# HGRN decay levels in a decoder step: from full 128x128 score blocks to the blocks that each mask keeps

## The reference, cut to what matters

```
def step(s, blk):
    qc, kc, vc, gc = blk
    b = jnp.cumsum(gc, axis=1)
    dec = jnp.exp(jnp.where(causal, b[:, :, None] - b[:, None, :], -jnp.inf))
    att = jnp.einsum('bthk,bshk,btshk->bhts', qc, kc, dec)
    o = jnp.einsum('bhts,bshv->bthv', att, vc) + jnp.einsum('bthk,bhkv->bthv', qc * jnp.exp(b), s)
    ...
```

## Time and profile before

| what | value |
|---|---|
| median of three runs | 3149.97 us (3140.21 to 3153.35) |
| the profiled execution | 3146.2 us |
| its span | 3144.4 us |
| mean granted TensorE clock | 0.949 |
| TensorE matmul busy | 2903.4 us (92%) |
| VectorE busy | 1385.3 us (44%) |
| ScalarE busy | 1325.0 us (42%) |
| all HGRN heads | from about 490 to 862 us of the span |

### The profile page before, as it was taken

One profiled execution on the slowest core, in us unless ns is written; L12 is line 12 of the kernel. 1 busy time (PEld: TensorE's weight loads), 2 busy tenths in 40 slices (PEclk: granted clock), 3 DMA queues, 4 the chain that ended last, 5 costly groups with the idle time before them and its releaser, 6 DMA issues.

```text
span 3144.4 us, 56333 instructions
## 1 busy us (share of the span) xinstructions
PE 2903.4 (92%) x22503; PEld 2465.3 (78%) x22503; DVE 1385.3 (44%) x2546; ACT 1325.0 (42%) x1798; POOL 40.4 (1%) x74
## 2 busy tenths in 40 slices
PE   5999997999899989899998999998989889899996
PEld 3899876888778867699887899876866557789996
DVE  2444237777655554544424444332124443454433
ACT  2554335555322225555434554332123334465542
POOL 0000000000000000000000000000000000000000
PEclk8999998999899889999999999999999998999998
DMA  6223441222112214222352223431355534322221
GB/s 232 87 101 123 171 153 48 74 72 78 64 57 83 90 57 170 93 103 95 114 189 98 81 93 120 171 132 60 109 161 154 171 98 181 127 81 93 98 93 64
DMA packets 58216, 349.21 MB, mean 111 GB/s; under 512 B 7473, under 2 KB 7810, under 8 KB 28546
## 3 DMA queue, kind: packets, MB, share of 16 engines
q1 hardware_dynamic: 52274, 322.85, 29.2%
q0 software_dynamic: 5840, 24.93, 2.2%
HBM read 335.30 MB, written 12.45 MB: 111 GB/s over the span
## 4 chain that ended last, share of the span: by engine, by line
PE 84%; DVE 8%; ACT 3%; DVEq 2%; issue 2%; DMA 1%; ACTq 0%; SPq 0%; POOL 0%
PE PS L815 53%; PE PS L780 10%; PE PS L829 2%; PE PS L983 2%; PE PS L797 2%; PE PS L1206 1%; PE PS L1188 1%; PE PS L1191 1%; PE PS L1167 1%; PE PS L853 1%; PE PS L948 1%; DMA weight_ring<-in_ada_w 1%; PE PS L1198 1%; DVE arena L2093 1%; PE PS L837 1%
## 5 line engine op out<-in xcount | busy, mean ns | idle before, releaser
L1719 DVE TENSOR_TENSOR w_rest<-weight_ring,w_hi 128x1024 bf16<-128x1024 f32 (+1 forms) x304 | 363.6, 1197 | 871.6 <-ACT w_hi L1370 866.5
L1370 ACT ACTIVATE w_hi<-weight_ring 128x1024 fp32r<-128x1024 f32 (+1 forms) x304 | 315.3, 1037 | 852.5 <-PE PS L815 844.6
L815 PE MATMUL PS<-hid_hi,w_hi 128*128 128x260 f32 x2688 | 363.4, 288 | 2.1 <-ACT w_hi L1370 2.1
L815 PEld LDWEIGHTS PS<-hid_hi,w_hi 128*128 128x128 f32 x2688 | 332.6, 189 | 5.5 <-issue 3.2
L815 PE MATMUL PS<-hid_rest,w_bf 128*128 128x260 bf16 x2688 | 329.7, 275 | 0.0
L815 PE MATMUL PS<-hid_bf,w_rest 128*128 128x260 bf16 x2688 | 327.8, 274 | 0.0
L1371 ACT ACTIVATE w_bf<-weight_ring 128x1024 bf16<-128x1024 f32 (+1 forms) x304 | 309.1, 1017 | 0.0
L815 PEld LDWEIGHTS PS<-hid_bf,w_rest 128*128 128x128 bf16 x2688 | 260.4, 97 | 40.3
L815 PEld LDWEIGHTS PS<-hid_rest,w_bf 128*128 128x128 bf16 x2688 | 247.1, 97 | 43.3
L780 PE MATMUL PS<-hidden,weight_ring 128*128 128x260 f32 x896 | 206.2, 393 | 12.8 <-ACTq L524 8.9
L780 PEld LDWEIGHTS PS<-hidden,weight_ring 128*128 128x128 f32 x896 | 175.5, 197 | 42.3 <-ACTq L524 9.3
(11 more groups left out here) (400 smaller groups left out, 4157.5 us busy)
## 6 DMA issues: line engine op xcount, KB each, us to landing
weight_ring<-in_ffn_gu SPq DMA_DIRECT2D x88, 1024.0 KB, 4.8
ada_chunks<-in_ada_w SPq DMA_DIRECT2D x40, 1536.0 KB, 6.6
weight_ring<-in_ffn_wd SPq DMA_DIRECT2D x32, 1408.0 KB, 5.9
weight_ring<-in_w_hgrn SPq DMA_DIRECT2D x16, 1024.0 KB, 4.8
weight_ring<-in_ada_w SPq DMA_DIRECT2D x8, 1536.0 KB, 8.1
weight_ring<-in_w_ssm SPq DMA_DIRECT2D x8, 1536.0 KB, 6.5
weight_ring<-in_mla_pairs SPq DMA_DIRECT2D x8, 1536.0 KB, 6.5
weight_ring<-in_w_out_ab SPq DMA_DIRECT2D x8, 1024.0 KB, 8.1
```

The lines of the kernel that those rows point to most:

```text
L815: last = pe.matmul(PS[:, bank + hf, 0:HT], w[:, buf, k * P:(k + 1) * P], x[:, first + k, hf * HT:(hf + 1) * HT], start=start and w is w_hi ...
L1370: act.activation(hi[:, buf, 0:n], src, ACT.Copy).then_inc(w_hi_ready, 1)
L1719: tt(WL_[:, buf, 0:n], W[:, slot, j * DC * P:j * DC * P + n], WH[:, buf, 0:n].bitcast(F32), ALU.subtract).then_inc(w_rest_ready, 1)
```

## The change

Level m of a chunk keeps only keys of a first half and queries of a second half. The changed kernel multiplies those blocks and no others. Level 64 is one block of 64 keys by 64 queries per chunk, level 32 is two blocks of 32 by 32, and both are full, so DVE copies them into AT with no mask. The diagonal and the levels 16 to 1 lie inside the four 32x32 blocks on the diagonal of the chunk. These are multiplied one by one, put side by side as 32 columns per chunk (128 columns in all in place of 512), and merged in a compact tile AB with compact masks; four copies spread AB over AT at the end. AT is zeroed once before the loop over heads.

```diff
-    masks = np.zeros((P, len(LEVELS), P), np.int32)
-    s, u = r[:, None], r[None, :]
+    masks = np.zeros((P, len(LEVELS), QR_), np.int32)
+    s, u = r[:, None], r[:, None] // QR_ * QR_ + r[None, 0:QR_]
...
+        AB = Arena(PARTS, _WIDTH[1] + len(LEVELS) * QR_).take(NCH, QR_)
...
+                        lhs, rhs = (KK, QS) if n == 0 else (DL[:, n - 1, :], DL[:, n - 1, :])
+                        m = LEVELS[n - 1] if n in (1, 2) else QR_
                         for c in range(NCH):
-                            cc = slice(c * CH, (c + 1) * CH)
-                            lhs, rhs = (KK[:, cc], QS[:, cc]) if n == 0 else (DL[:, n - 1, cc], DL[:, n - 1, cc])
-                            last = pe.matmul(PS[:, n % 2, cc], lhs, rhs, start=True, stop=True)
+                            for at in range(0, CH, 2 * m if n in (1, 2) else m):
+                                keys = c * CH + at
+                                queries = keys + m if n in (1, 2) else keys
+                                col = queries if n in (1, 2) else c * QR_
+                                last = pe.matmul(PS[at:at + m, n % 2, col:col + m], lhs[:, keys:keys + m],
+                                                 rhs[:, queries:queries + m], start=True, stop=True)
...
+                dve.memset(AT, 0.0)
...
                         dve.wait_ge(h_p, h * 8 + (n + 1))
-                        src = PS[:, n % 2, :].rearrange("p (a b) -> p a b", a=NCH)
+                        if n in (1, 2):
+                            m = LEVELS[n - 1]
+                            for at in range(0, CH, 2 * m):
+                                last = dve.tensor_copy(
+                                    AT[at:at + m, :, at + m:at + 2 * m],
+                                    PS[at:at + m, n % 2, :].rearrange("p (a b) -> p a b", a=NCH)[:, :, at + m:at + 2 * m])
+                            last.then_inc(h_ptk, 1)
+                            continue
+                        src = PS[:, n % 2, 0:NCH * QR_].rearrange("p (a b) -> p a b", a=NCH)
                         if n == 0:
-                            tt(AT, src, ident, ALU.mult).then_inc(h_ptk, 1)
-                            dve.drain()
+                            tt(AB, src, bcast(const("fold")[:, 0:QR_], 1, NCH), ALU.mult).then_inc(h_ptk, 1)
                         else:
                             apart(dve)
-                            dve.copy_predicated(AT, bcast(MSK[:, n - 1, :], 1, NCH), src).then_inc(h_ptk, 1)
-                            dve.drain()
-                    dve.sem_inc(h_att, 1)
+                            dve.copy_predicated(AB, bcast(MSK[:, n - 1, :], 1, NCH), src).then_inc(h_ptk, 1)
+                        dve.drain()
+                    for at in range(0, CH, QR_):
+                        dve.tensor_copy(AT[at:at + QR_, :, at:at + QR_], AB[at:at + QR_])
+                    dve.drain().then_inc(h_att, 1)
```

More of the change, by code:

```diff
@@ L201, in build_program @@
              ("gate", [P, 2, T], F32)],
-            [("mixer_consts", [P, _WIDTH[1]], F32), ("level_masks", [P, len(LEVELS), P], I32)])
+            [("mixer_consts", [P, _WIDTH[1]], F32), ("level_masks", [P, len(LEVELS), QR_], I32)])
         BIG, (GH_, GB, GL, MST), (_, OCH, OCB, SQ), (_, GHH, _, GHB, GHL, GWL) = shared(
@@ L1901, in head @@
                         cut(h, QUERY, 1)
-                    ident = bcast(IDENT, 1, NCH)
                     for n in range(1 + len(LEVELS)):
                         dve.wait_ge(h_p, h * 8 + (n + 1))
-                        src = PS[:, n % 2, :].rearrange("p (a b) -> p a b", a=NCH)
+                        if n in (1, 2):
[7 more added lines that the diff above has]
+                        src = PS[:, n % 2, 0:NCH * QR_].rearrange("p (a b) -> p a b", a=NCH)
                         if n == 0:
-                            tt(AT, src, ident, ALU.mult).then_inc(h_ptk, 1)
-                            dve.drain()
+                            tt(AB, src, bcast(const("fold")[:, 0:QR_], 1, NCH), ALU.mult).then_inc(h_ptk, 1)
                         else:
                             apart(dve)
-                            dve.copy_predicated(AT, bcast(MSK[:, n - 1, :], 1, NCH), src).then_inc(h_ptk, 1)
-                            dve.drain()
-                    dve.sem_inc(h_att, 1)
+                            dve.copy_predicated(AB, bcast(MSK[:, n - 1, :], 1, NCH), src).then_inc(h_ptk, 1)
[3 more added lines that the diff above has]
+                    dve.drain().then_inc(h_att, 1)
                     dve.wait_ge(s_loaded, h * 16 + 16)
```

## The result

| | before | changed |
|---|---|---|
| median of 6 runs | 3145.46 us | 3124.85 us |
| lowest to highest | 3140.21 to 3153.35 | 3119.6 to 3130.01 |
| ratio changed/before | | 0.9925, interval 0.9914 to 0.9936 |
| profiled execution, its span | 3146.2, 3144.4 | 3130.01, 3128.2 |
| granted clock, mean | 0.949 | 0.943 |

The changed kernel is faster by 0.75%, 23.6 us by the ratio. The forecast was 3120 us, from a sum of 28 us. The profiled execution of the changed kernel is the slowest of its six, so its span is some 5 us above what its median would show.

The account below looks back on a forecast made before the run. TensorE, busy 92%, was taken to set the pace; four heads 3.24 us and four 3.75 us earlier, less 0.3 for zeroing, made 28 us, so 3118.5, moved to 3120 us for a low profiled run; range 3104 to 3146.

Parts of the forecast that it names:

- a sum of 28 us: Sample states start 3.24 us earlier in four heads, 3.75 in four, less 0.3 us for zeroing AT.
- Strips: TensorE's 32x32 products on four strips: 13.8 ns per pair, a level 0.44 us in place of 1.04.
- The rival of 31 ns: TensorE's pairs come no closer than in one strip, a level costs 1.0 us; 3140 us in all, chance 0.19.
- VectorE's pieces: VectorE's copies: masked 0.33 us, n = 0 0.28, level 64 0.42, level 32 0.45, four at the end 0.7.
- Pace of the levels: Between TensorE and VectorE, levels follow each other every 0.54 us in place of 1.04.
- a bank's round trip: Refill, product and masked copy take 1.08 us per turn of one PSUM bank; two banks give 0.54 us per level.
- The wait behind FORGET: After the FORGET projection TensorE still waits for VectorE's chunk states, 1.0 to 1.5 us per head.
- The heads at full clock: Four heads, worked on the third: n = 0 starts as before at 617.47, sample states start 3.24 us earlier.
- clock lost: Granted clock falls to 0.50 at the levels and stays through FORGET: 22 us slower, 3168 us; chance 0.08.
- My count of four changes per head: TensorE's tiling mode changes four times per head, each draining it; no row isolated the cost.

Follow-up runs that it names:

- pe_blocks_wide_dve: Kernel before with only TensorE's part of the change (kept blocks multiplied in their old places); VectorE still masks 512 columns: 3150.9 us, ratio 1.0009 to before.
- one_wait: Changed kernel with eight products side by side in three banks, one VectorE wait for all, chunk states behind them: 3146.89 us, ratio 0.9993 to before.
- double_tiles: Changed kernel with the products of levels 16 to 1 multiplied twice: 3135.2 us, ratio 0.9958 to before.
- n0_tiles_only: Kernel before with only n = 0 multiplied in 32x32 blocks: 3155.35 against 3148.08 us, ratio 1.0020.
- filler_before_states: Changed kernel with eight unread bf16 matmuls before the chunk states' wait for ACT's copy of KD: 3126.13 us, ratio 0.9932 to before.
- one_wait_filler_all: one_wait with 7 and 6 unread matmuls in the value-transpose gaps and 22 before the wait for the states: 3110.9 us, ratio 0.9876 to before.

## Why the prediction was right, and where its steps were not

**Strips: right.** A level of 32 pairs was to cost 0.44 us, between 0.22 and 2.1. It costs 0.35 us from the first load to the end of the last, so about 8 ns from pair to pair, and 8.6 ns when 64 follow each other. The rival of 31 ns is refuted. The sentence of the Trainium skill ("TensorE: Matmul & The Clock Gate", Wait — 56ns, not 53.3ns?) that starts come no closer than about 25 ns does not hold across strips here.

**VectorE's pieces: nearly right.** Masked copy 0.30 (0.33 forecast), n = 0 0.29 (0.28), level 64 0.42 (0.42). Low were the two copies of level 32, 0.58 (0.45), and the four at the end, 0.92 (0.7, bounds 0.6 to 1.1).

**Pace of the levels: right number by luck.** 0.57 us against 0.54. I built it from a bank's round trip (1.08 us in two banks). With the measured pieces that sum is 0.05 + 0.35 + 0.22 + 0.04 + 0.30 = 0.96, or 0.48 us per level. The pace is 0.30 of copy and 0.27 of VectorE's own, as pe_blocks_wide_dve shows; one_wait shows that a drain makes up 0.075 of it. It follows that a quicker TensorE or a third bank alone should have brought nothing; neither was run. But the bank's turn is close behind: double_tiles, with 0.3 us more of TensorE, was slower.

**The wait behind FORGET: right in kind.** 1.0 to 1.5 us forecast, 1.64 to 1.65 measured in each of the first seven heads, 18.6 us over all heads in place of 14.2. FORGET ran at 1.00, as forecast.

**The heads at full clock: the step that failed.** I wrote of the third head that VectorE "starts at 617.47 as before", and so took TensorE to come up to the levels at the clock that it had had. It didn't: the clock falls during L969, which takes 3.46 us in place of 2.05, and the chunk states take 2.07 in place of 1.16. From the start of L969 to the end of level 64's copy I had 6.43 us for this head; it took 8.33. The sixth and the seventh took 7.86 and 8.30 where the same working gives 6.45 and 6.85. The eighth, at the lower clock for a shorter time, took 6.87 where it gives 6.97. That is 4.7 us in all. The heads 1, 2, 4 and 5 took what the forecast had in this part, within 0.2 us.

The other 3.5 us of the miss lie in VectorE's part, in all eight heads: from the end of level 64's copy to the sample states I had 4.30 us, and they took 4.60 to 4.95. In the fourth head the level 32 copies, the pace and the four copies at the end make 0.24, 0.16 and 0.24 of it. In sum the forecast of 28 us became 19.8.

Why the clock goes is known in part. The narrower n = 0 alone is enough (n0_tiles_only). The wait behind it, from 0.74 to 1.23 us where n = 0 still runs at full clock, is not what comes first: in the changed kernel the clock falls before that wait in seven heads, and in filler_before_states it falls with the wait filled. What ties a shorter n = 0 to a fall that mostly stands ahead of it is open.

The rival "clock lost" did happen, though not where I had put it: it asked for FORGET at half clock and 8 slower heads, and what it cost was 1.4 to 1.9 us in three heads. That idle time of TensorE can carry the lower clock into the large products is shown by one_wait with and without its fillers; pe_blocks_wide_dve fits it. One step further and it eats the whole gain.

**A cost that I left out.** The weight loads pause for 0.17 and 0.22 us ahead of n = 0 and of n = 1, with "issue" as the reason, where tiles of 128 give way to narrower ones; these gaps are not in the kernel before. The Trainium skill ("TensorEngine Tiling (Array Packing)", Key Properties) says that a change of tiling mode drains TensorE, and these rows agree in kind. Not every change shows it: in one_wait_filler_all the loads go from tiles of 32 to tiles of 64 after 0.04 us (567.79 to 567.83). The two gaps are about 0.4 us per head on TensorE; what exactly a drain takes of it was not isolated. (My count of four changes per head was one short: 128 to 32 for n = 0, back for the chunk states, then 64, 32 and 128 again.)

**Why the time still lay near the forecast.** The runs gave 23.6 us by the ratio (20 to 27 by its interval), the head-by-head account 19.8. The difference is within the scatter of single executions, of which the trace shows one and a slow one. So it is in part luck that a sum that was off by 8.2 us in the heads came within 5 us of the time: 4 us of the gain stand in no part that the sum accounts for.

Still open: what in VectorE's step of one level makes up the 0.2 us beside the drain (wait, register or semaphore increments); it was removed only as a whole. Also whether real work in TensorE's gaps, in place of unread matmuls, keeps the clock; no such order was tried.

## What to carry to other kernels

When an engine is made faster, ask first what it will wait for next, and on TensorE also what the clock does around it: n = 0 alone in small tiles made this kernel slower by 0.2%, the whole change made it faster by 0.75%, and the same change with one wait of VectorE and three of TensorE's waits filled by 1.24%. Read where the clock falls head by head before you name a cause: the wait that is easy to see in one head stood behind the fall, not ahead of it. When two engines alternate and both show idle time, do not take it for granted that they wait for each other: look whether the releaser says "issue", and price each step of the consumer with its wait and signal (0.27 us here) beside its work (0.30 us). A small gain per step from fewer waits is worth more than the arithmetic: eight waits turned into one, with the products side by side, brought the sample states 2 us forward, which paid only once TensorE's wait was filled.

## What the runs showed of the hardware that I had not expected

- Four strips of 32x32 fp32 pairs start about 8 ns apart over 32 pairs and 8.6 ns over 64.
- Chunk states of eight fp32 matmuls take 1.16 us at a granted clock of 1.00 and 2.08 us at 0.50. With only n = 0 narrower, all eight heads had 2.08 us, and in six of them the clock fell before that n = 0.
- Eight unread bf16 matmuls in the wait behind n = 0 halved the time at 0.50 there (about 3.5 us in place of 7); the clock still fell, in two heads while they ran.
- Unread bf16 matmuls shorten the kernel one_wait: 0.9993 became 0.9897 with 22 per head, and 0.9876 with 35.
- Masked copies of 128 columns: 0.075 us apart with a drain, 0.27 us with drain, wait and semaphore increments.
